# The Toeplitz matrix of a state-space layer in four 128-partition transfers, with fewer warm products behind them

## The reference

```python
abar = exp(lambda * step)                       # complex, 64 groups x 64 states
bbar = f * b                                    # 64 groups x 64 states x 16 channels
bu[l] = u[l] @ bbar                             # u = the normed input, 16 channels a group
x[l] = abar * x[l - 1] + bu[l]                  # over the 256 positions
y[l] = Re(C x[l]) + d * u[l]
out = a * sigmoid(g),  a, g = split(gelu(y) @ w_out)
```

## Time and profile before

| | us |
|---|---|
| median of 3 runs | 858.52 (858.01 to 859.07) |
| the profiled execution | 859.13 |
| its span, first to last instruction | 857.4 |
| PE busy | 687.7 (80%) |
| DVE, ACT, POOL busy | 189.6, 127.2, 189.6 |
| chain that ended last: PE, DMA, DVE | 47%, 35%, 7% |
| of it `DMA ub<-xn` | 3% |
| granted TensorE clock, mean | 0.911 |

### The profile page before, as it was taken

How to read it: one execution, slowest core, us unless ns; L and a number is a source line. 1 busy time by engine, 2 the same in 40 slices (tenths; PEclk the granted TensorE clock), 3 DMA queues, 4 the chain that set the end, 5 groups by cost and what they waited for, 6 DMA issues and landing times.

```text
span 857.4 us, 12011 instructions
## 1 busy us (share of the span) xinstructions
PE 687.7 (80%) x5209; PEld 410.3 (48%) x5209; DVE 189.6 (22%) x421; ACT 127.2 (15%) x274; POOL 189.6 (22%) x234
## 2 busy tenths in 40 slices
PE   7999989898898886895553859998789979577564
PEld 4778877564453454462321444445454435244231
DVE  2131331442032120021032190135002202001004
ACT  1043233120010110011010212012201101001001
POOL 3000301525995920510884000000000000000000
PEclk9999999999898898897875989999989989899787
DMA  9986222758996999999999885234599799999981
GB/s 309 346 215 201 99 99 86 290 97 364 421 422 258 425 421 419 422 421 422 419 256 119 202 260 222 98 117 202 217 421 420 311 423 419 421 421 420 421 372 50
DMA packets 73721, 256.13 MB, mean 299 GB/s; under 512 B 15536, under 2 KB 45328, under 8 KB 47168
## 3 DMA queue, kind: packets, MB, share of 16 engines
q1 hardware_dynamic: 70816, 246.27, 75.9%
q0 software_dynamic: 2064, 7.93, 3.1%
q10 hardware_dynamic: 784, 1.09, 0.7%
HBM read 249.02 MB, written 5.20 MB: 297 GB/s over the span
## 4 chain that ended last, share of the span: by engine, by line
PE 47%; DMA 35%; DVE 7%; SPq 4%; issue 3%; ACT 2%; POOL 2%; DVEq 0%; ACTq 0%; POOLq 0%
DMA ring<-in_moe_w_down 16%; DMA ring<-in_moe_w_up 10%; PE ps L1538 8%; PE ps L1558 7%; PE ps L1733 7%; PE ps L1435 5%; PE ps L1307 5%; PE ps L1371 3%; DMA ub<-xn 3%; DMA ring<-in_moe_w_gate 3%; PE ps L1310 3%; PE ps L1569 2%; DMA ring<-in_attn_w_qkv 1%; DMA chunk_inputs<-stage 1%; SPq L351 1%
## 5 line engine op out<-in xcount | busy, mean ns | idle before, releaser
L1538 PE MATMUL ps<-ring,xg 128*32 128x256 f32 x2048 | 143.4, 443 | 60.8 <-DMA ring<-in_moe_w_gate 32.4
L1538 PEld LDWEIGHTS ps<-ring,xg 128*32 128x32 f32 x2048 | 82.9, 127 | 128.8 <-issue 104.9
L1558 PE MATMUL ps<-ring,hidT 128*32 128x512 f32 x528 | 80.1, 716 | 29.2 <-DMA ring<-in_moe_w_down 23.9
L1288 PE MATMUL ps<-ident,ones 128*128 128x512 f32 x108 | 53.6, 652 | 20.3 <-issue 17.4
L1109 DVE TENSOR_TENSOR hid<-sg,ps 128x256 f32<-128x256 f32 (+1 forms) x18 | 7.6, 420 | 245.2 <-ACT sg L814 245.2
L1569 PE MATMUL ps<-y_sb,pickT 128*128 128x512 f32 x128 | 59.0, 604 | 2.8 <-DVE y_sb L1118 2.8
L1307 PE MATMUL ps<-xnT,ring 128*128 128x256 f32 x256 | 57.6, 382 | 2.4 <-DMA ring<-in_attn_w_qkv 1.7
L1435 PE MATMUL ps<-pick,xn 128*128 128x256 f32 x256 | 58.6, 383 | 0.2
L1733 PE MATMUL ps<-ring,yT 128*128 128x512 f32 x128 | 56.3, 595 | 2.4 <-ACT yT L879 1.8
L1558 PEld LDWEIGHTS ps<-ring,hidT 128*32 128x32 f32 x528 | 20.2, 128 | 77.0 <-issue 69.0
L1307 PEld LDWEIGHTS ps<-xnT,ring 128*128 128x128 f32 x256 | 47.8, 190 | 10.4 <-issue 2.4
(11 more groups left out here) (297 smaller groups left out, 716.6 us busy)
## 6 DMA issues: line engine op xcount, KB each, us to landing
ring<-in_moe_w_down SPq DMA_DIRECT2D x66, 1024.0 KB, 19.0
ring<-in_moe_w_gate SPq DMA_DIRECT2D x66, 1024.0 KB, 18.1
ring<-in_moe_w_up SPq DMA_DIRECT2D x66, 1024.0 KB, 18.5
ring<-in_attn_w_qkv SPq DMA_DIRECT2D x11, 1024.0 KB, 12.0
ring<-in_ssm_w_out SPq DMA_DIRECT2D x8, 1024.0 KB, 11.5
ring<-in_attn_w_o SPq DMA_DIRECT2D x4, 1024.0 KB, 5.7
ring<-kernel_lags SPq DMA_DIRECT2D x8, 512.0 KB, 22.2
chunk_inputs<-stage POOLq DMA_DIRECT2D x3, 1024.0 KB, 9.2
```

The lines of the kernel that those rows point to most:

```text
L1288: mm(ps[:, bank, :], ones[:], ident[:].unsqueeze(1).to_broadcast([P, 4, P]), start=True, stop=True)
L1538: ins = mm(ps[CAP * h:CAP * (h + 1), GUB, F * half:F * (half + 1)], p.xg[:, c, CAP * (ROUND * r + h):CAP * (ROUND * r + h + 1)], w, start= ...
L1558: ins = mm(ps[CAP * h:CAP * (h + 1), DNB + b, :], hidT[:, r, j, CAP * h:CAP * (h + 1)], w, start=(j == 0), stop=(j == FT - 1), tile_positi ...
```

## The change

The eight transfers of the Toeplitz read become four, one for each ring slot. Each writes all 128 partitions, 8 KB each, and reads with a pattern of its own: 8 positions one row apart, 16 channels 15 rows apart, 2048 floats in a row. With a positive step over the positions, partition group m now holds the rows from m on, which is position Q-1-m: the positions of a chunk lie on the partitions in falling order. To match, `uq` is filled from `ub[:, ::-1]` (both copies), and POOL's chunk-input matrices take the powers in rising order. PE waits for four transfers in place of eight. The warm products before the wait for `uq` go from 20 to 6.

```diff
-WARM = {"start": 6, "norm": 7, "choice": 5, "ranks": 2, "state-space norm": 20, "loads": 0}
+WARM = {"start": 6, "norm": 7, "choice": 5, "ranks": 2, "state-space norm": 6, "loads": 0}
...
-            for m in range(Q):
-                sp.dma_start(ring[GC * m:GC * (m + 1), :, GU:SLOT],
-                             k_dram[:, Q - 1 - m:2 * Q - 1 - m, :].rearrange("c (s l) n -> c s (l n)", l=2)).then_inc(toe_loaded, 16)
+            for s in range(RING):
+                lags = bass.AP(tensor=k_dram.tensor, offset=2 * s * D, ap=[[D, Q], [(2 * Q - 1) * D, GC], [1, 2 * D]])
+                sp.dma_start(ring[:, s, GU:SLOT], lags).then_inc(toe_loaded, 16)
...
-                ar, ai = (apw[:, r, 0:Q, mine][:, ::-1, :].rearrange("p l s -> p s l").unsqueeze(3).to_broadcast([P, 8, Q, GC])
+                ar, ai = (apw[:, r, 0:Q, mine].rearrange("p l s -> p s l").unsqueeze(3).to_broadcast([P, 8, Q, GC])
...
-                           ub[:, :, P:2 * P].rearrange("p m (j c) -> p m j c", c=GC)).then_inc(u_evac_a, 1)
+                           ub[:, ::-1, P:2 * P].rearrange("p m (j c) -> p m j c", c=GC)).then_inc(u_evac_a, 1)
...
-                          ub[:, :, 0:P].rearrange("p m (j c) -> p m j c", c=GC)).then_inc(u_evac_d, 1)
+                          ub[:, ::-1, 0:P].rearrange("p m (j c) -> p m j c", c=GC)).then_inc(u_evac_d, 1)
...
-            pe.wait_ge(toe_loaded, 16 * Q)
+            pe.wait_ge(toe_loaded, 16 * RING)
```

## The result

The changed kernel takes 862.88 us (median of 20 runs, 859.09 to 868.38) against 858.65 us for the kernel before (20 runs): ratio 1.005, 95% interval 1.0034 to 1.0067. The forecast was 846 us, with 836 to 859.5 as range; the measured time lies outside it, on the side of rival C. The profiled execution has a span of 860.9 us against 857.4.

The account below looks back on a forecast made before the run. The prediction took the slow Toeplitz transfers, with ub queued behind them, to bound the kernel between the layers. Terms -15.1 (earlier uq) and +2.65 (cold PE) gave -12.4; 859.13 - 12.4 - 0.6 = 846 us, range 836 to 859.5.

Parts of the forecast that it names:

- rival C: Toeplitz read: partition groups meet on the same ports, rate stays about 117 GB/s, kernel slower at 860 us; chance 0.20.
- The rate of the read (part 1): Toeplitz read: four 1 MB transfers, carried by 8 of 16 DMA engines, run at 210 GB/s and take 19.9 us.
- The ub transfers (part 2): Before uq: ACT's transfers cost the read 3.3 us, SP's land 4.35 us after it; uq starts at 468.2, -15.1 us.
- The branch (part 3): PE's branch before the warm products: its 11 us excess shrinks to 3 to 6 us, PE back between 455.4 and 458.5.
- The clock (part 3): PE's transposes and input products start at 1.2 GHz after idling: +2.65 us, bounds 0 and +5.3.
- The order of positions (part 4): Copies from ub read backwards into uq, and POOL's powers in rising order: 0 us, bounds 0 and +1.1.
- No time of its own later: Everything after uq is released from that point, so a gain or loss there reaches the end whole.
- theory N: From the experiments, rival C generalized: read rate follows from SBUF ways (fixed partition groups) written at once, about 29 GB/s each.

Follow-up runs that it names:

- before_ub_waits: The kernel before, with SP and ACT issuing the ub transfers only when the eight Toeplitz transfers have landed: 865.26 us, ratio 1.0065.
- ub_waits: The changed kernel, with SP and ACT issuing the ub transfers only when the Toeplitz matrix has landed: 862.88 us, ratio 1.0056.
- lag_major: The changed kernel with k_dram laid out lag by lag, so each transfer's source counts 128 outermost: 839.75 us, ratio to before 0.977.
- before_warm6: The kernel before with 6 warm products in place of 20, nothing else: 856.77 us, ratio 0.9989.
- channel_outer: The changed kernel with partitions as (channel, position) in the read, uq and chunk-input matrices, source counting 16 outermost: 842.97 us, ratio 0.983.
- eight_apart: The changed kernel with the read as sixteen transfers of 32 partitions, outermost count 8, rows misordered so output is wrong: 850.02 us, single run.

## Why the prediction was wrong, step by step

**The rate of the read (part 1): this step failed, and it is most of the error.** The prediction took "the middle, half of 421: 210 GB/s, 19.9 us", from 8 engines alone. The engines were counted rightly (share 0.51) but a share of engines isn't a rate: it was 121 GB/s, 34.6 us for the 4.19 MB. `uq` came 20.4 us later than forecast (488.6 for 468.2); 14.7 of them are this term, and the rest is in the main the next part's. I had the second factor in rival C and gave it 0.20, with "against it: eight groups are written at once, where it was one" as the reason.
**The ub transfers (part 2): this step failed too.** The part counted 3.3 us for ACT's transfers and 4.35 us behind the last lag. "4.35 us after the last lag" was read rightly from before and was not a property of `ub`: 5 us of its time lay beside the old read. Alone it takes 10.7 to 10.8 us from its first issue (before_ub_waits, ub_waits, lag_major). This is what makes the change slower and not just neutral, and neither my forecast nor rival C had it. In 457 to 468 the free half of the engines lets `ub` in early, and the sum falls to 94 GB/s where the earlier trace rows show 132 with both. That the mix is worse there is measured; how the ways share it among 1 KB and 8 KB pieces is argued only. The "about 1 us of latency" behind the 3.3 us has no row either; the shortest landing of a `ub` transfer in these runs took 3.4 us.

**The branch (part 3): shorter than forecast, and not for the reason given.** The sum had PE back between 455.4 and 458.5, a branch of 6.5 to 9.6 us, because the read would be faster. It took 3.7 us, and the read was as slow as before. In before_warm6, with 16 engines at 117 GB/s, it takes 14.1 us, in channel_outer, 16 at 236, 9.0, in lag_major, 16 at 412, 5.9, and in eight_apart, 8 at 217, 4.8. So with all 16 engines busy it does shrink as the rate grows, and with half of them free it is short even beside the slow read.

**The clock (part 3): the state right, the price wrong.** The transposes began at 0.50 as said, 1.3 to 1.7 us longer. The +2.65 us at the end are at most 1 us (before_warm6), and the stage is even shorter. The sum priced the start alone; in the kernel before the stage started warm, then lost 2.47 us in a gap and fell to clock 0.50 from 493 to 496. So in rival C, too, the loss came from another place than I had put it: its 860 us were made of the clock, the measured 862.9 are made of `ub`.

**The order of positions (part 4): right.** ACT's copy took 1.05 us, DVE's 0.69, as before.

**No time of its own later: right.** From the first GLU product to the end it is 342.3 to 345.7 us in all eleven profiles.

## What to carry to other kernels

In these runs a transfer over all 128 partitions was fast only where, by theory N, its engines write different parts of SBUF at the same moment: look at both the DMA share and the GB/s, since share 0.5 can go with 121 or with 217. What worked here was to give both sides a single outermost step over the partitions, by laying out the DRAM tensor for it (lag_major: 412 GB/s and 2.3% of the kernel, against a loss of 0.5% for the same four transfers without it). And the time from one transfer's landing to the next one's is not the second one's own time; take away the overlap before it is used in a sum.

## What the runs showed of the hardware that I had not expected

Half of the engines cost nothing as long as the ways were the bound (117 with 16, 121 with 8), and PE's branch was short beside them: it took 3.7 us beside the 8-engine read, 14.4 beside the 16-engine read of the same rate. That this is PE fetching its code is the prediction's guess, and no run tests it. Eight 128 KB transfers inside SBUF, each into 16 partitions, take 10.7 us together from the first issue to the last landing, about 98 GB/s; in lag_major's chain they still hold 7.6 us ahead of `uq`. A stage of short dependent products that began at half clock ended no later than the one that began warm (28.6 us in before_warm6, 30.8 in the kernel before); in both the granted clock fell to 0.50 again inside the stage.
